# The slot list of a mixture-of-experts layer as one-hot products on TensorE, and a mixer's input rounded and split per token tile from PSUM

## The reference, cut to what matters

```python
def trunk(x, ...):
    for layer in range(2):
        h = delta_pool_mixer(x, ...) if layer == 0 else rglru_mixer(x, ...)
        x = layer_norm(ALPHA * x + h, ...)
        f = moe(x, router_w, router_bias, w_gate[layer], w_up[layer], w_down[layer])
        x = layer_norm(ALPHA * x + f, ...)

def moe(x, ...):                       # 16 experts in 4 groups; each token gets 2 of the best group
    scores = sigmoid(x @ router_w); biased = scores + router_bias
    combine = two best experts of the best group, weights scores / their sum
    for e in range(16):
        y += combine[:, e] * ((silu(x @ w_gate[e]) * (x @ w_up[e])) @ w_down[e])

def rglru_mixer(x, ...):
    y_br, x_br = split(x @ w_in)       # 1024 -> 2 x 1024
    xc = causal_conv(x_br) ; r, gi = sigmoid(block_diagonal(xc)) ; h = scan(a(r), sqrt(1-a*a) * gi * xc)
    return (h * gelu(y_br)) @ w_out
```

## Time and profile before

| | |
|---|---|
| median of three runs | 1488.68 us |
| the profiled execution | 1487.37 us, of which span 1485.4 us |
| busy share of the span | PE 83%, PEld 67%, DVE 64%, ACT 47%, POOL 17% |
| the experts' two stages | from 511.19 and from 1143.51 us (first products) |
| the second mixer's first product | 867.27 us |
| granted TensorE clock, mean | 0.895 of 2.4 GHz |

### The profile page before, as it was taken

The page is one execution under the profiler, slowest core; times in us unless marked ns, Lnnn a source line. Parts: engine busy times, 40 slices in busy tenths (PEclk is TensorE's granted clock), DMA queues, the critical chain, the costliest instruction groups (busy, mean ns, idle before and its releaser), DMA issues. The chain is left out here.

```text
span 1485.4 us, 16270 instructions
## 1 busy us (share of the span) xinstructions
PE 1230.4 (83%) x6413; PEld 997.2 (67%) x6413; DVE 954.2 (64%) x1185; ACT 704.6 (47%) x813; POOL 256.4 (17%) x267
## 2 busy tenths in 40 slices
PE   7999878878996299999994179899962999999940
PEld 6989877855444288888883179785442888888830
DVE  4864345433255389998993956553552999989838
ACT  4433222221013187888882343570131878788832
POOL 3431432202000400000002300351004000000023
PEclk9999989995897599999997579999975999999985
DMA  5211220010713299999993601122152999999932
GB/s 163 88 57 57 67 82 1 1 50 1 255 43 135 67 378 422 415 415 414 414 363 126 203 29 58 57 103 92 51 220 60 386 413 413 414 414 414 372 131 89
DMA packets 78349, 294.56 MB, mean 198 GB/s; under 512 B 10160, under 2 KB 36489, under 8 KB 53696
## 3 DMA queue, kind: packets, MB, share of 16 engines
q1 hardware_dynamic: 65728, 250.50, 43.8%
q0 software_dynamic: 7936, 26.23, 4.9%
q10 hardware_dynamic: 4608, 16.78, 2.8%
HBM read 266.59 MB, written 26.90 MB: 198 GB/s over the span
## 5 line engine op out<-in xcount | busy, mean ns | idle before, releaser
L2023 DVE TENSOR_TENSOR UNIT_LOW<-work,UNIT_HIGH 128x2048 fp32r<-128x2048 f32 x192 | 436.2, 2290 | 55.5 <-ACT UNIT_HIGH L1176 55.2
L1176 ACT ACTIVATE UNIT_HIGH<-work 128x2048 fp32r<-128x2048 f32 x192 | 365.7, 1919 | 82.6 <-PE bank L1035 82.6
L1033 PE MATMUL bank<-UNIT_HIGH,XGT_HIGH 128*128 128x512 f32 x512 | 204.4, 399 | 5.0 <-DVE XGT_LOW L2030 5.0
L1035 PE MATMUL bank<-UNIT_HIGH,XGT_LOW 128*128 128x512 f32 x512 | 201.1, 393 | 0.0
L1034 PE MATMUL bank<-UNIT_LOW,XGT_HIGH 128*128 128x512 f32 x512 | 200.6, 392 | 0.0
L1176 ACT ACTIVATE work<-bank 128x512 f32<-128x512 f32 (+4 forms) x180 | 75.3, 472 | 117.5 <-PE bank L717 29.8
L1033 PEld LDWEIGHTS bank<-UNIT_HIGH,XGT_HIGH 128*128 128x128 f32 x512 | 97.2, 190 | 25.0 <-DVE XGT_LOW L2030 5.8
L1035 PEld LDWEIGHTS bank<-UNIT_HIGH,XGT_LOW 128*128 128x128 f32 x512 | 96.9, 189 | 21.0
L1034 PEld LDWEIGHTS bank<-UNIT_LOW,XGT_HIGH 128*128 128x128 f32 x512 | 97.2, 190 | 19.4
L2352 POOL DMA_INDIRECT work<-x_rows,idx_all x32 | 30.9, 964 | 430.5 <-PE bank L1027 420.8
L1033 PE MATMUL bank<-UNIT_HIGH,HT_HIGH 128*128 128x512 f32 x256 | 99.7, 390 | 3.4 <-DVE HT_LOW L2042 3.4
(11 more groups left out here) (457 smaller groups left out, 2618.9 us busy)
## 6 DMA issues: line engine op xcount, KB each, us to landing
work<-in_moe_w_gate_dram SPq DMA_DIRECT2D x64, 1024.0 KB, 7.4
work<-in_moe_w_up_dram SPq DMA_DIRECT2D x64, 1024.0 KB, 7.7
work<-in_moe_w_down_dram SPq DMA_DIRECT2D x64, 1024.0 KB, 8.0
y_rows<-work ACTq DMA_DIRECT2D x32, 512.0 KB, 7.9
work<-in_ab_w_in_dram SPq DMA_DIRECT2D x10, 1024.0 KB, 5.3
work<-in_c_w_in_dram SPq DMA_DIRECT2D x8, 1024.0 KB, 5.6
x_rows<-X SPq DMA_DIRECT2D x8, 512.0 KB, 2.6
X<-in_x_prompt_dram SPq DMA_DIRECT2D x4, 512.0 KB, 5.3
```

Of the source, the lines that this page charges most:

```text
L1033: mm(to, x[0], high, start=start, stop=False)
L1035: return mm(to, x[1], high, start=False, stop=stop)
L1176: return nc.scalar.activation(out, in_, ACT.Copy, scale=scale)
L2023: V.tensor_tensor(UNIT_LOW[home(l, n)][:, :], work[:, UNIT * home(l, n):UNIT * home(l, n) + UNIT], UNIT_HIGH[(NU * l + n) % HIGHS][:, :].b ...
```

## The change

Two parts. **The slot list** is no longer scattered to DRAM and read back. VectorE makes `SLOT_HOT` (for each choice and token tile, a row of 128 with a one at the token's rank) and `TOK_HOT` (the one-hot experts times the token number), and ten products on TensorE, 128x16 each, sum them in a PSUM bank: the result at row s, column e is the token in slot s of expert e. VectorE copies it to `idx_all`, and the gathers wait for that copy (`idx_ready`). `pos_i`, still needed for gathering the results, and the largest count come after it; the ten scatters and the read-back stand in the overflow branch. **The second mixer's input** is rounded (ScalarE) and split (VectorE) per tile straight from PSUM, tiles 0 and 1 inside `norm(1)`, the others in front of `mixer1` with the first two weight blocks between them; `XT` is not written there. The histories are transposed ahead of the tiles and copied behind them. SyncE loads two blocks of `c_w_in` before the gate weights, and a third one and the LayerNorm weights after the sums of `norm(1)`. The results of token tile 4 and the history rows get other addresses. GpSimd makes a 128 wide iota and a float copy of the token numbers at the start.

```diff
@@ SyncE
-                sp.wait_ge(tok_scattered, 160 * (l + 1))
-                sp.dma_start(idx_all[:, :, :], slot_list[l].rearrange("(b s e) o -> s b (e o)", b=BLOCKS, s=P))\
-                  .then_inc(idx_in, 16)
...
+                sp.wait_ge(norm_sum, 2 * NT)
+                load_w(2)
+                lnp(0, 1, ln_mix_g, ln_mix_b)
@@ TensorE, to_channels
+                    if t >= 2 and n == 2:
+                        split1.wait(pe, 0, f"x{t - 2}")
@@ TensorE, out_and_route
+                for k in range(2):
+                    pe.wait_ge(slot_hot, 2 * l + k + 1)
+                    for t in range(NT):
+                        last = mm(bank[3][:, 0:NE], SLOT_HOT[0:ROWS[t], k, t, :], TOK_HOT[0:ROWS[t], k, t, :],
+                                  start=(k == t == 0), stop=(k == 1 and t == NT - 1))
+                last.then_inc(idx_ps, 1)
@@ ScalarE
                     if t:
                         scaled(t - 1)
+                    if q == 1 and t >= 3:
+                        x1_rounded(t - 3)
                 scaled(NT - 1)
+            def x1_rounded(t):
+                act.wait_ge(xt_ps, 2 * NT + t + 1)
+                b, cols = TILE_BANK(t), tile_cols(t)
+                copy(XT_HIGH[:, 0:4, cols], heads_of(b, P, ROWS[t]))
+                rounded1.end(copy(XT_HIGH[:, 4:8, cols], heads_of(b + 1, P, ROWS[t])), 0, f"x{t}")
@@ ScalarE, mixer1
+                x1_rounded(2)
                 round_w(0)
-                act.wait_ge(lru_hist_out, 3)
-                for t in range(NT):
-                    act.wait_ge(xt_lo, 2 * NT + t + 1)
-                    act.wait_ge(xt_hi, 2 * NT + t + 1)
-                    rounded1.end(copy(XT_HIGH[:, :, tile_cols(t)], XT[:, :, tile_cols(t)]), 0, f"x{t}")
                 round_w(1)
+                x1_rounded(3)
+                x1_rounded(4)
@@ VectorE
+                    if q == 1 and t >= 3:
+                        x1_split(t - 3)
                 finish(NT - 1)
+            def x1_split(t):
+                rounded1.wait(dve, 0, f"x{t}")
+                b, cols = TILE_BANK(t), tile_cols(t)
+                V.tensor_tensor(XT_LOW[:, 0:4, cols], heads_of(b, P, ROWS[t]), XT_HIGH[:, 0:4, cols].bitcast(F32), ALU.subtract)
+                split1.end(V.tensor_tensor(XT_LOW[:, 4:8, cols], heads_of(b + 1, P, ROWS[t]),
+                                           XT_HIGH[:, 4:8, cols].bitcast(F32), ALU.subtract), 0, f"x{t}")
@@ VectorE, route
+                mine(V.tensor_tensor(TOK_HOT, oh, tok_f[:, :].unsqueeze(1).unsqueeze(3).broadcast_to([P, 2, NT, NE]), ALU.mult))
...
-                V.tensor_copy(pos_i[:, :, :], rt[:, 6:8, 0:NT]).then_inc(pos_ready, 1)
+                dve.wait_ge(state_out, 16 * 8)
+                for k in range(2):
+                    V.tensor_tensor(SLOT_HOT[:, k, :, :], iota128[:, :].unsqueeze(1).broadcast_to([P, NT, P]),
+                                    rt[:, 6 + k, 0:NT].unsqueeze(2).broadcast_to([P, NT, P]), ALU.is_equal)\
+                        .then_inc(slot_hot, 1)
...
+                dve.wait_ge(idx_ps, l + 1)
+                V.tensor_copy(idx_all[:, 0, :], bank[3][:, 0:NE]).then_inc(idx_ready, 1)
+                do(V.tensor_reduce(rt[:, 5, 0:1], rt[:, 4, 0:NE], AX.X, ALU.max))
+                do(V.tensor_copy(over_i[:, :], rt[0:1, 5, 0:1]))
+                V.tensor_copy(pos_i[:, :, :], rt[:, 0:2, 0:NT]).then_inc(pos_ready, 1)
@@ VectorE, mixer1
+                x1_split(2)
+                split_w(0)
+                split_w(1)
+                x1_split(3)
+                x1_split(4)
                 dve.wait_ge(lru_hist_ps, 1)
...
-                split_w(0)
-                for t in range(NT):
-                    rounded1.wait(dve, 0, f"x{t}")
-                    split1.end(V.tensor_tensor(XT_LOW[:, :, tile_cols(t)], XT[:, :, tile_cols(t)],
-                                               XT_HIGH[:, :, tile_cols(t)].bitcast(F32), ALU.subtract), 0, f"x{t}")
-                split_w(1)
@@ GpSimd, constants and experts
+                for i in range(1, P // NE):
+                    mine(G.tensor_scalar(iota128[:, NE * i:NE * i + NE], iota16, float(NE * i), None, ALU.add))
+                do(G.tensor_copy(tok_f[:, :], tok_id[:, :]))
...
+                pool.wait_ge(idx_ready, l + 1)
                 pool.wait_ge(state_out, 16 * 8)
-                pool.wait_ge(idx_in, 16 * (l + 1))
```

More of the change, by code:

```diff
@@ L122, in hybrid_trunk @@
         inv_cnt = sb("inv_cnt", [P, 16])
-        iota16 = sb("iota16", [P, NE])
+        iota128 = sb("iota128", [P, P])
+        iota16 = iota128[:, 0:NE]
+        tok_f = sb("tok_f", [P, NT])
         m_lower4 = sb("m_lower4", [P, 4, 4])
@@ L282, in landed @@
             return 16 * (l * loads[n % RING] + n // RING + 1)
-        Y1, Y2 = ([work[:, 12288 + D * (2 * t + k):13312 + D * (2 * t + k)] for t in range(NT)]
-                  for k in range(2))
+        SLOT_HOT = view(24576, (2, NT, P))
+        TOK_HOT = view(28416, (2, NT, NE))
+        Y_AT = [12288 + 2 * D * t for t in range(NT - 1)] + [4096]
+        Y1, Y2 = ([work[:, at + D * k:at + D * k + D] for at in Y_AT] for k in range(2))
         own = {e: sem(f"{e}_own") for e in ("dve", "pool")}
@@ L356, in hybrid_trunk @@
         ysel_scaled = sem("ysel_scaled")
-        operands = ["w0"] + [f"x{t}" for t in range(NT)] + [f"w{c}" for c in range(1, 16)]
+        operands = ["x0", "x1", "x2", "w0", "w1", "x3", "x4"] + [f"w{c}" for c in range(2, 16)]
         rounded1, split1 = steps("rounded1", operands), steps("split1", operands)
@@ L368, in ov_wait @@
             who, per_step, at = OV[part]
-            start = 4 if who == "pe" else 0
+            start = {"pe": 4, "xg": 16 * (2 * NT + 1)}.get(who, 0)
             engine.wait_ge(ov[l][who], n * per_step + (at - per_step + start))
@@ L399, in samples, with copied_low, copied_high @@
             return ap[:, TP:T].rearrange("p (s l) -> p s l", s=NS)
+        def copied_low(n, t):
+            return {0: 0, 1: NT, 3: 2 * NT}[n] + t + 1
+        def copied_high(n, t):
+            return {1: 2 * NT, 3: 3 * NT}[n] + t + 1
         def at_least(engine, s, value):
@@ L478, in mixer1, with load_w @@
                       .then_inc(hist1_in, 16)
+                win = c_w_in[0].rearrange("(k p) c -> p k c", p=P)
+                def load_w(n):
+                    c = (D + 256 * n) % (2 * D)
+                    sp.dma_start(W0[n % 3], win[:, :, c:c + 256]).then_inc(w_in[n % 3], 16)
+                load_w(0)
+                load_w(1)
                 for n, src in enumerate((c_w_r, c_w_i)):
                     sp.dma_start(WRI[:, n, :, :], src[0].rearrange("h (k p) j -> p (h k) j", p=P)).then_inc(wri_in, 16)
-                win = c_w_in[0].rearrange("(k p) c -> p k c", p=P)
-                for n in range(8):
-                    if n >= 3:
-                        sp.wait_ge(proj1_ps, 2 * (n - 3) + 2)
-                    c = (D + 256 * n) % (2 * D)
-                    sp.dma_start(W0[n % 3], win[:, :, c:c + 256]).then_inc(w_in[n % 3], 16)
+                sp.wait_ge(norm_sum, 2 * NT)
+                load_w(2)
+                lnp(0, 1, ln_mix_g, ln_mix_b)
+                for n in range(3, 8):
+                    sp.wait_ge(proj1_ps, 2 * (n - 3) + 2)
+                    load_w(n)
                 wout = c_w_out[0].rearrange("(k p) d -> p k d", p=P)
@@ L2016, in route @@
                 mine.settle()
-                V.tensor_copy(pos_i[:, :, :], rt[:, 6:8, 0:NT]).then_inc(pos_ready, 1)
+                dve.wait_ge(state_out, 16 * 8)
[3 more added lines that the diff above has]
+                        .then_inc(slot_hot, 1)
+                do(V.scalar_tensor_tensor(per(3, NE), per(3, NE), float(NE),
+                                          iota16.unsqueeze(1).broadcast_to([P, NT, NE]), ALU.mult, ALU.add))
+                for k in range(2):
+                    mine(V.tensor_tensor(per(8 + k, NE), per(3, NE), oh[:, k, :, :], ALU.mult))
+                mine.settle()
+                for k in range(2):
+                    mine(V.tensor_reduce(rt[:, k, 0:NT], per(8 + k, NE), AX.X, ALU.add))
+                dve.wait_ge(idx_ps, l + 1)
[3 more added lines that the diff above has]
+                V.tensor_copy(pos_i[:, :, :], rt[:, 0:2, 0:NT]).then_inc(pos_ready, 1)
             def experts(l):
@@ L2354, in gather @@
                         in_offset=bass.IndirectOffsetOnAxis(ap=idx_all[:, 0, e:e + 1], axis=0)).then_inc(xg_in[e % 2], 16)
-                pool.wait_ge(lists_zeroed, 32)
-                pool.wait_ge(pos_ready, l + 1)
-                for t in range(NT):
-                    for k in range(2):
-                        pool.indirect_dma_start(
-                            out=slot_list[l], in_=tok_id[0:ROWS[t], t:t + 1], in_offset=None,
-                            out_offset=bass.IndirectOffsetOnAxis(ap=pos_i[0:ROWS[t], k, t:t + 1], axis=0),
-                        ).then_inc(tok_scattered, 16)
+                pool.wait_ge(idx_ready, l + 1)
```

(12 more changed lines are left out.)

70 lines of the change are left out of this document (30 added, 40 removed).

## The result

The changed kernel takes 1449.89 us (median of 4 runs, 1446.9 to 1450.28) beside 1489.85 us of the kernel before on the same chip: a ratio of 0.9729, interval 0.9707 to 0.975, 40.0 us less. On a second chip it was 1448.71 against 1487.65: 0.9737 (0.9724 to 0.9751). The forecast was 42.0 us less and 1446.7; the time lies inside the range of 1441 to 1455, 3.2 us above the forecast. The first interval is 37 to 44 us, so the medians alone can't tell a miss of 2 us.

A forecast was written before the change was run, and what follows sets the result against it. The critical path runs almost all through TensorE, and what can be won is where it stands still. Savings of 14.8 + 15.5 + 11.7 = 42.0 us from the median 1488.68 give 1446.7 us, range 1441 to 1455.

The forecast's parts named there:

- Three stretches of one critical path, savings that add: Both layers' routes to the first expert product and the second mixer's start: 14.8 + 15.5 + 11.7 = 42.0 us less.
- The ten products, 3.1 us a layer: TensorE's one-hot list products: 20 records of 16 columns at 0.155 us, bounds 0.094 and 0.246 a record.
- `SLOT_HOT`, `TOK_HOT`, the repeated arithmetic: VectorE: `SLOT_HOT` comparisons 0.82 us each, second and repeated place arithmetic beside TensorE; `TOK_HOT` about 0.32 within a 0.73 wait.
- VectorE's splits late next, the gather hidden: Before the first expert product: VectorE's five weight splits end last, hiding 3.4 us of the gather's saving.
- The third rival: Experts' start: gather starts late after GpSimd's long rest; if it lost 7 us, total 1453.9; chance 0.08.
- The route's sum: Slot list to first expert product: 14.8 us less in layer 0, 15.5 less in layer 1.
- The mixer's start, 11.7 us: End of `norm(1)` to second mixer's projection: first product at 855.6 instead of 867.27, 11.7 us less.
- The second rival: Second mixer's earlier start gains nothing at the end, only the route counts: 1458.4 us; chance 0.06.
- Two early splits free in `norm(1)`: Splits of tiles 0 and 1, 1.29 us each, fall where VectorE stands behind GpSimd's bias, costing nothing.
- The first rival: In `norm(1)` GpSimd stops the PSUM subtractions, so both early splits add 2.6 us: 1449.3; chance 0.10.
- GpSimd's constants, taken as 0: Start-up: seven small operations and a copy, 0.8 to 2.3 us against 2.04 free; cost 0 to 0.3.
- the fourth rival: Experts' stages: with less rest TensorE's granted clock falls; at 0.90 the time would be 1506.7 us; chance 0.01.

The follow-up runs named there:

- the halves apart: Slot-list part alone, and second-mixer part alone, each put into the kernel before: 1461.07 and 1476.24 us, beside 1485.67 for the kernel before.
- the mixer alone: Kernel before with only the second mixer's input part of the change, without the slot-list part: 1476.24 us, ratio 0.9935.
- the products twice: Changed kernel with the ten one-hot products of a layer run twice into the same bank: 1458.59 us.
- the kernel with idle work: Changed kernel with idle float32 products of 512 columns on TensorE, six behind the last logits, three behind the rank products: 1444.77 us.

## Why the prediction was right, and the term that was mis-sized

- **Three stretches of one critical path, savings that add.** Right: 39.7 us at the three places, and the halves apart show the same intervals.
- **The ten products, 3.1 us a layer.** This is the term that was wrong: 4.78 us, 1.7 more per layer, just inside the bound of 0.246 a record. The nearest row was misread. The count behind a stretch in the earlier trace rows is of all records that overlap it; I took it as records begun. Counted by their starts, the logits at the lower clock are 18 records between 460.8 and 464.4 us in the trace before, 0.21 us each:

```profile
L979 PE MATMUL bank<-rw,XT x18: 374/374/374, 460.8 to 464.4; 128*128 128x16 f32 x18
```

  (a line's records in a stretch: durations of one, least, median and most, in ns, then the first and the last start). That would have made 4.2 us; the rest to 4.78, some 0.5, is not explained. The lower bound of 0.094 came from the same misreading; at clock 1.00 a record of these products was measured at 0.135 (2.70 / 20). The Trainium skill, "VectorE: DVE Perf Modes", section "The TRN2 errata", gave some 0.5 us for all ten as an estimate, 1.0 if each of the twenty records is counted; the trace disagrees, 4.78, and in its stretch the weight loads are busy 4.56 of the 4.78 us.
- **`SLOT_HOT`, `TOK_HOT`, the repeated arithmetic.** Right: two passes of 0.82 with overlap 1.56; `TOK_HOT` in the wait for the ranks, which shrank from 0.73 to 0.49.
- **VectorE's splits late next, the gather hidden.** Right, and tried: taking two splits off the way gave 3.7 and 3.2 us a layer. The third rival (a late gather after GpSimd's rest) falls: 103.02 us of rest, and a gather that starts 0.29 us behind the end of the list's copy, against 0.87 taken. The prediction has layer 1's DMA half a microsecond slower than layer 0's; from the gather's start to the transposes it took, in the trace before, 5.04 us (1134.03 to 1139.07), 0.79 more than layer 0's 4.25, which stayed in the cover too.
- **The route's sum.** 14.8 and 15.5 were 13.56 and 14.28, 2.5 us less in all. That is the products' 3.4 less some 0.9 that the smaller steps were cheaper, so a part of the error was covered by luck. The signs moved alike: the first expert product came 19.7 us behind the start of the rank addition (479.44) in both layers, where 18.5 were said, and the list's copy 6.8, where 5.5 were said. The medians lie on the same side (40.0 and 38.9 against 42.0), but their intervals are wider than this.
- **The mixer's start, 11.7 us.** Right: 11.87 by profile. The second rival (hidden at the end) falls with the mixer alone, 1476.24 against 1485.67. The parameter chain ran under the first projection block as said: VectorE was done with it at 846.36, and began the convolution that needs it at 854.28.
- **Two early splits free in `norm(1)`.** Right, and tried: 0.68 us beside GpSimd's bias. The first rival falls. By the Trainium skill, "GPSIMD Engine Reference", section "Specifications", contention needs two SBUF inputs or a two-port mode; these subtractions read PSUM and SBUF, and the trace agrees.
- **GpSimd's constants, taken as 0.** Nearly: where the inputs came early, in the run of the products twice, VectorE waited 0.42 us for the last constant and began at 16.41, against 16.16 before. In the changed kernel's two profiles it began at 18.53 and 17.64, but that was the third tile's arrival: its rounding on ScalarE began anywhere from 11.63 to 14.12 us in the twelve profiles of these kernels, at 12.16 before and at 13.28 with the mixer alone, which has no new constants. So the late start is probably no work of the change; one profile of the kernel before can't show it.
- **The clock in the experts' stages.** 1.00 over 270 us as before; the fourth rival falls.

## What to carry to other kernels

When a chain through memory is replaced by a few small products, price these at the clock that the waiting engine has in that stretch, and count records by their starts, not by the number that overlaps a stretch. After shortening one chain, look at once at what the other engine does first out of habit: here two of five splits stood in front of the operand that everything waited for, worth 7 us. Look also for places where an engine's operation stands for another engine: here two subtractions that read PSUM and SBUF ran at their own 0.68 us beside GpSimd's bias, where VectorE's next operation stood anyway, and cost nothing.

## What the runs showed of the hardware that was not expected

- A float32 product of 128 by 128 weights and 16 columns is two records of 0.239 us at clock 0.50; as fp32r it is one of 0.259. The weight loads were busy 4.56 of the 4.78 us of twenty records, and 2.42 of the 2.59 us of ten.
- The granted clock fell to the lower level amid the products with 16 columns, while TensorE was wholly busy (layer 0's ten products in the kernel with idle work, 1.00 and then 0.53). The 64 logits records of layer 1 took from 8.45 us (1.00 in their first half, 0.68 in the second) to 11.21 us (0.74 and 0.50) in twelve profiles of nearly the same code.
- During products that compute nothing, put into TensorE's rests, the granted clock rose to 1.00 and stood there when the expert began; they were worth some 6 us in a kernel of 1437, between two chips.
- A VectorE operation on 64x1 elements stood 2.33 us beside GpSimd's bias; with two PSUM subtractions in front of it it took 1.14, and nothing was lost.
